# One-hot products of the mixture layers split into a rounded part and a rest, and three modulation parts of the third mixer summed on the vector engine

## The reference

```python
cond = jax.nn.silu(c)
for i in range(DEPTH):                     # layers 2 and 3 of the kernel
    sh1, sc1, g1, sh2, sc2, g2 = jnp.split(cond @ ada_w[i] + ada_b[i], 6, axis=-1)
    h = modulate(rmsnorm(x, norm_mix_g[i]), sh1, sc1)
    mix = gla_mixer(h, ...) if i % 2 == 0 else lru_mixer(h, ...)
    x = x + g1[:, None] * mix
    h = modulate(rmsnorm(x, norm_ffn_g[i]), sh2, sc2)
    x = x + g2[:, None] * grouped_moe(h, ...)

def grouped_moe(...):                      # combine: 2 of 16 experts per token
    for e in range(N_EXPERTS_2):
        he = jax.nn.silu(t @ w_gate[e]) * (t @ w_up[e])
        out = out + combine[:, e:e + 1] * (he @ w_down[e])
```

## Time and profile before

| | us |
|---|---|
| median of three runs | 2803.23 |
| lowest, highest | 2800.44, 2810.59 |
| the profiled execution: whole time | 2816.16 |
| its span, first to last instruction | 2814.4 |
| mean granted TensorE clock, of 2.4 GHz | 0.927 |
| third mixer, first slot to last modulation piece | 1744 to 1867 |
| mixture of layer 2, first gate product to last add | 1975 to 2291 |
| mixture of layer 3, the same | 2476 to 2801 |

### The profile page before, as it was taken

One profiled execution on the slowest core, in us unless ns is written; L12 is line 12 of the kernel. 1 busy time (PEld: TensorE's weight loads), 2 busy tenths in 40 slices (PEclk: granted clock), 3 DMA queues, 4 the chain that ended last, 5 costly groups with the idle time before them and its releaser, 6 DMA issues.

```text
span 2814.4 us, 26206 instructions
## 1 busy us (share of the span) xinstructions
PE 2422.6 (86%) x9674; PEld 1281.0 (46%) x9676; DVE 1169.7 (42%) x2825; ACT 625.0 (22%) x1780; POOL 644.9 (23%) x823
## 2 busy tenths in 40 slices
PE   6999888787778989977787788987999988799998
PEld 2577433333333567433333334346454456544544
DVE  0326666766664336667766763023100022320001
ACT  1112323322233122323332333111110022110101
POOL 1103433333332102433343331100222000012100
PEclk7989998899999999999899899987999999799999
DMA  8748999999997757999999997853899135579970
GB/s 328 301 171 332 416 421 422 421 422 421 421 422 314 286 207 312 417 422 421 422 421 422 421 421 328 312 204 135 359 421 421 70 135 201 247 307 421 421 299 16
DMA packets 130128, 934.40 MB, mean 332 GB/s; under 512 B 14288, under 2 KB 16336, under 8 KB 16592
## 3 DMA queue, kind: packets, MB, share of 16 engines
q0 software_dynamic: 114768, 835.96, 72.1%
q1 hardware_dynamic: 15232, 96.75, 8.8%
HBM read 1070.02 MB, written 1.05 MB: 381 GB/s over the span
## 4 chain that ended last, share of the span: by engine, by line
PE 54%; DMA 26%; DVE 15%; ACT 4%; issue 1%; SPq 0%; DVEq 0%; ACTq 0%
PE units L1101 15%; PE units L645 13%; DMA arena<-rows,idx 11%; PE accs L887 11%; DMA wide<-rows,idx 8%; DMA ring<-stream 5%; PE units L1079 3%; PE accs L1146 3%; DVE wide L1804 3%; DVE arena L1804 2%; PE units L660 2%; PE accs L725 2%; DMA wide<-experts 2%; ACT arena L1331 1%; DMA arena<-ada 1%
## 5 line engine op out<-in xcount | busy, mean ns | idle before, releaser
L887 PE MATMUL accs<-wide,arena 128*128 128x512 f32 x1040 | 518.7, 654 | 146.7 <-ACT arena L1331 144.9
L887 PE MATMUL accs<-arena 128*128 128x512 f32 x1008 | 482.7, 633 | 93.2 <-ACT arena L1331 93.2
L887 PEld LDWEIGHTS accs<-wide,arena 128*128 128x128 f32 x1040 | 211.3, 208 | 438.2 <-issue 254.3
L555 POOL DMA_INDIRECT wide<-rows,idx x260 | 245.0, 942 | 602.1 <-PE accs L887 422.0
L1101 PE MATMUL units<-wide,arena 128*64 128x512 f32 (+1 forms) x1728 | 368.1, 597 | 8.4 <-DMA wide<-experts 6.0
L887 PEld LDWEIGHTS accs<-arena 128*128 128x128 f32 x1008 | 203.1, 205 | 369.9 <-issue 248.8
L1199 ACT ACTIVATE arena<-units 128x512 f32<-128x512 f32 (+2 forms) x204 | 111.2, 559 | 1017.0 <-PE units L645 312.7
L645 PE MATMUL units<-arena,ring 128*128 128x256 f32 (+1 forms) x1344 | 300.2, 386 | 28.3 <-ACT arena L1226 14.0
L555 POOL DMA_INDIRECT arena<-rows,idx x252 | 237.3, 942 | 359.9 <-PE accs L887 322.1
L645 PEld LDWEIGHTS units<-arena,ring 128*128 128x128 f32 x1344 | 256.3, 200 | 74.2 <-issue 38.6
L1101 PE MATMUL units<-arena 128*64 128x512 f32 (+1 forms) x960 | 232.7, 593 | 0.5 <-ACT arena L1199 0.5
(11 more groups left out here) (301 smaller groups left out, 2102.1 us busy)
## 6 DMA issues: line engine op xcount, KB each, us to landing
wide<-experts POOLq DMA_DIRECT2D x123, 1024.0 KB, 13.4
wide<-experts SPq DMA_DIRECT2D x93, 1024.0 KB
wide<-ada POOLq DMA_DIRECT2D x88, 1024.0 KB, 9.2
arena<-experts POOLq DMA_DIRECT2D x69, 1024.0 KB, 16.2
ring<-stream SPq DMA_DIRECT2D x62, 1024.0 KB, 6.8
arena<-experts SPq DMA_DIRECT2D x51, 1024.0 KB
arena<-side SPq DMA_DIRECT2D x8, 1024.0 KB, 8.2
wide<-ada SPq DMA_DIRECT2D x7, 1024.0 KB, 16.9
```

What stands on the lines that cost most here:

```text
L555: pool.indirect_dma_start(row_slot(i), None, rows[l], bass.IndirectOffsetOnAxis(ap=idx[:, n, k:k + 1], axis=0)).then_inc(row_sem(i), 16)
L887: ins = mm(o[:, half * 512:(half + 1) * 512], diag[:, i % (2 * GROUP), :], row_slot(PICKS * l + i)[:, D + half * 512:D + (half + 1) * 512] ...
```

## The change

1. **Modulation parts of the third mixer.** `added(DEPTH)` names the three parts that PE took in `gla`. `add_piece` on DVE now multiplies each piece by its scalar of `cact` and adds it up in `ada_sums` (one tensor_scalar, then seven scalar_tensor_tensor of 2048 columns for each part), and a memset of one column releases the ring place. PE reads the sum with four matmuls against `one` (`sum_added`), after the first and second value pairs and after the gates. Parts 1 and 2 on DVE wait until PE has read the part before, since there is one `ada_sums`. That buffer is the seventh place: `ADA_RING` is 6 for every layer.
2. **One-hot products.** Tokens and the experts' results are stored as an f32r part (ACT writes it, rounded) and the rest, x minus that part (f32r too). The rest of the tokens is subtracted on POOL, between its 11th and 12th expert load; that of the results on DVE, in place of the copy. `place` and `add` run on both parts in f32r, so with twice as many matmuls, and `place` takes two tiles at a time: 32 matmuls of 256 columns at every second tile, into four units.
3. **The combine weight** goes into `h` (DVE's product becomes a scalar_tensor_tensor with a per-place scalar). The scalar comes from two one-column matmuls with `back` as weights; the scatter matrix is now `to` turned by two f32r matmuls against `ident_r`, not `back` by transposes. ACT takes both and does so one tile earlier than the tile that uses them (`turn_back(p + 1)`).

The diff, cut to its core:

```diff
-ADA_RING = 7
+ADA_RING = 6
+def added(l):
+    return ((l, 1), (l, 2), (l + 1, 0)) if l == DEPTH else ()
@@ POOL
             def expert_loads(l):
-                pool.wait_ge(ada_read, after_of(l))
+                for i in range(after_of(l) - ADA_RING, after_of(l)):
+                    pool.wait_ge(ada_free(i), ada_uses(i))
+                pool.wait_ge(ada_summed, sums_before(l + 1))
                 for i in range(OWN):
+                    if i == NE:
...
+                            pool.wait_ge(tok_hi_ready, 2 * TB * (l - DEPTH) + n + 1)
+                            wait_taken(pool, u)
+                            g.tensor_tensor(tok_lo[:, b, cut], tok[:, b, cut], tok_hi[:, b, cut].bitcast(F32),
+                                            ALU.subtract).then_inc(tok_lo_ready, 1)
@@ PE
+            def sum_added(l, j):
+                which, part = added(l)[j]
+                pe.wait_ge(ada_added, KT * (sums_before(l) + j + 1))
+                for g in range(4):
+                    ins = mm(ada_bank(which, part)[32 * g:32 * g + 32, :], one[:, 0:1].broadcast_to([P, 32]),
+                             ada_sums[:, g * 512:(g + 1) * 512], start=True, stop=True, skip_group_check=True)
+                ins.then_inc(ada_summed, 1)
-                token_slots(SLOT_OF["gk", l], UNIT_OF["gk", l], hT, adas=2)
+                token_slots(SLOT_OF["gk", l], UNIT_OF["gk", l], hT)
                 for c in range(2):
-                    token_slots(SLOT_OF["gv", l] + 2 * c, UNIT_OF["gv", l] + 2 * c, hT, adas=2)
+                    token_slots(SLOT_OF["gv", l] + 2 * c, UNIT_OF["gv", l] + 2 * c, hT)
+                    sum_added(l, c)
...
+                sum_added(l, 2)
+                def place(q):
+                    at = batch_tiles(q) * P
+                    for c, u in enumerate(batch_units(l, q)):
+                        open_bank(u)
+                        for j in range(2):
+                            k = 2 * c + j
                             for b in range(TB):
+                                for part, tok in enumerate(toks):
+                                    ins = mm(bank(u)[:, j * T:(j + 1) * T], tok[:, b, k * P:(k + 1) * P],
+                                             to[:, b, at:at + 2 * P], start=b + part == 0, stop=b + part == TB)
+                def turn_back(p):
+                    u = tile_units(l, p)["back"]
+                    open_bank(u)
+                    for b in range(TB):
+                        mm(bank(u)[:, b * P:(b + 1) * P], to[:, b, p * P:(p + 1) * P], ident_r[:, :], start=True, stop=True)
+                    for b in range(TB):
+                        ins = mm(bank(u)[:, T:T + 1], back[:, b, p * P:(p + 1) * P], one[:, :], start=b == 0, stop=b == TB - 1)
@@ add
                     for d in range(KT):
-                        ins = mm(acc[d // 2][:, (d % 2) * T:(d % 2 + 1) * T], o[:, d * P:(d + 1) * P], bT, ...)
+                        for part, o in enumerate(os):
+                            ins = mm(acc[d // 2][:, (d % 2) * T:(d % 2 + 1) * T], o[:, d * P:(d + 1) * P], bT, ...)
@@ the order on PE
-                for i in range(2 * TB):
-                    wait_taken(pe, UNIT_OF["tokens", l] + i)
+                pe.wait_ge(tok_lo_ready, 2 * TB * (l - DEPTH + 1))
                 pe.wait_ge(spread_ready, TB * (l - DEPTH + 1))
                 place(0)
+                pe.wait_ge(back_ready, l - DEPTH + 1)
+                turn_back(0)
...
+                    if p % 2 and p + 1 < TILES:
+                        place((p + 1) // 2)
                     if p + 1 < TILES:
-                        place(p + 1)
-                    transposes(q["back"], [back[:, b, p * P:(p + 1) * P] for b in range(TB)])
+                        turn_back(p + 1)
                     down(p)
@@ ACT
+                    for c, u in enumerate(q["down"]):
+                        wait_full(act, u)
+                        af(o_hi[:, c * 512:(c + 1) * 512], bank(u)[:, :], ACT.Copy).then_inc(o_hi_ready, 1)
@@ DVE
+            def add_piece(l, j, k):
+                if k == 0 and j:
+                    dve.wait_ge(ada_summed, sums_before(l) + j)
+                n = i - ADA_FIRST
+                dve.wait_ge(ada_landed[n % ADA_RING], 16 * (n // ADA_RING + 1))
+                if k == 0:
+                    ts(ada_sums, ada_piece(i), w, None, ALU.mult).then_inc(ada_added, 1)
+                else:
+                    stt(ada_sums, ada_piece(i), w, ada_sums, ALU.mult, ALU.add).then_inc(ada_added, 1)
+                v.memset(psr[:, k:k + 1], 0.0).then_inc(ada_free(i), 1)
-                    took(tt(h, si, bank(q["up"])[:, :], ALU.mult), q["up"])
+                    took(stt(h, si, wgt[:, p % 2, 0:1], bank(q["up"])[:, :], ALU.mult, ALU.mult), q["up"])
-                        took(v.tensor_copy(o[:, c * 512:(c + 1) * 512], bank(u)[:, :]), u)
+                        dve.wait_ge(o_hi_ready, 2 * (TILES * (l - DEPTH) + p) + c + 1)
+                        took(tt(o_lo[:, cut], bank(u)[:, :], o_hi[:, cut].bitcast(F32), ALU.subtract), u)
```

More of the change, by code:

```diff
@@ L66, with _tile_plan, take @@
 SIDE = (2, 3, 4, 5)
+BATCHES = (TILES + 1) // 2
+def _tile_plan():
+    n = 0
+    at = [{} for _ in range(TILES)]
+    batch = []
+    def take(k):
+        nonlocal n
+        n += k
+        return tuple(range(n - k, n))
+    batch.append(take(4))
+    at[0]["back"], = take(1)
+    for p in range(TILES):
+        (at[p]["gate"],), (at[p]["up"],), (at[p]["turn"],) = take(1), take(1), take(1)
+        if p % 2 and p + 1 < TILES:
+            batch.append(take(4))
+        if p + 1 < TILES:
+            at[p + 1]["back"], = take(1)
+        at[p]["down"] = take(2)
+    return at, batch, n
+TILE_AT, BATCH_AT, TILE_UNITS = _tile_plan()
 def plan():
@@ L138, in pieces, with sums_before, ada_uses @@
     return ((l, 1), (l, 2)) + (((l + 1, 0),) if l + 1 < LAYERS else ())
+def added(l):
+    return ((l, 1), (l, 2), (l + 1, 0)) if l == DEPTH else ()
+def sums_before(l):
+    return sum(len(added(n)) for n in range(l))
+def ada_uses(i):
+    return (i - ADA_FIRST) // ADA_RING + 2
 def before_of(l):
@@ L714, in ada_slots @@
             def ada_slots(n):
-                for i in range(ada_at[0], ada_at[0] + n):
+                todo = [i for i in range(ada_at[0], LAYERS * ADA_SLOTS) if not any(
+                    (i // ADA_SLOTS, i % ADA_SLOTS // KT) in added(l) for l in range(LAYERS))][:n]
+                ada_at[0] = todo[-1] + 1 if todo else ada_at[0]
+                for i in todo:
                     l, part, k = i // ADA_SLOTS, i % ADA_SLOTS // KT, i % KT
@@ L1116, in hidden @@
                     q, loads = tile_units(l, p), tile_loads(p)
-                    for c in range(2):
-                        wait_taken(pe, q["place"][c])
+                    half = p % 2 * P
+                    for u in batch_units(l, p // 2):
+                        wait_taken(pe, u)
                     for name, first in (("gate", 0), ("up", 2)):
```

157 lines of the change are left out of this document (107 added, 50 removed).

## The result

The changed kernel takes 2791.16 us (median of 9 runs, 2785.08 to 2800.45) and the kernel before 2809.06 (9 runs, 2800.44 to 2818.49): a ratio of 0.9939, 95% interval 0.9919 to 0.9959. It is faster by 0.6%, about 17 us. The forecast said 34, so its direction held and its size was twice what came.

A forecast was written before the change was run, and what follows sets the result against it. PE bounds the third mixer, with ring loads close behind; DMA paces the mixture's own tiles, and PE is alone behind the last load. -14.6 - 3.5 - 16.2 = -34 off the median 2803.2 gives 2769, by itself 2757 to 2783.

The forecast's parts named there:

- Part 3: Mixture of layers 2 and 3: one-hot products in f32r, 0.12 us per matmul of 256 columns; gain 16.2 in both.
- Costed at nothing: POOL's four subtractions: Head of the mixture: at most 5.2 us, ending at 1965, covered because PE waits for DVE until 1968.9.
- if PE waits at the head of the mixture for POOL's subtractions: Sign in the new profile, at the mixture's head, that the forecast is wrong altogether; no size given.
- Part 2: Modulation ring of six places: gain 3.5 us (0 to 4) in layer 1, together 0 in layer 3.
- one MB less is 2.5 us less: Start of layer 1: PE's wait of 2.67 nearly goes and the slot of 8.77 returns to 7.13; gain 3.5.
- Part 1: Third mixer: modulation parts moved from PE to DVE, stage from 122.6 to 108.0 us; gain 14.6.
- about 11 with a slower clock in one or two: Third mixer: five ring slots fall into the DMA backlog, 2 to 3 us each.
- The second reading: Third mixer: PE's wait before it 1 to 2 us; longer than 3 would mean DVE's chain was mis-sized.
- (a): Rival, one-hot products: f32r loads weights as slowly as f32, an add takes 3.8, total 2799; chance 0.12.
- (b): Rival, one-hot products: f32r runs at f32's speed, an add takes 6.9, total 2943; chance 0.07.
- (c): Rival, third mixer: every slot waits for its ring load while DVE adds, 9.5 to 10.2 each; 2783; chance 0.09.
- (d): Rival, own tiles: PE's clock stays down after waits, costing 5 to 7 us a layer; 2781; chance 0.06.

The follow-up runs named there:

- mix_only: The changed kernel with the mixture's one-hot products alone: modulation pieces all on PE again, ring of seven places; ratio to the kernel before 0.9963.
- keys_late: The changed kernel with layer 1's keys (1 MB) loaded behind all its modulation pieces instead of ahead of them; 2789.0 us, ratio 0.9932.
- sum_early: The changed kernel with PE's first reading of a sum two slots earlier and the second two slots later; 2789.4 us, ratio 0.9927.
- pace3: sum_early with at most three of the third mixer's 24 modulation pieces under way instead of six; 2790.07 us, ratio 0.9937.

## Why the forecast was right in direction and wrong in size

- **Part 3, the tiles: right.** The forecast's -9.0 behind the last load (its -8.1 without the +0.9 of the head) was -8.9 and -7.5 in the changed kernel's profile, -9.0 and -8.9 in mix_only's. Its prices hold: an add 2.10 (forecast 1.9), a gather 3.84 (3.8), the turning 0.57 (0.7).
- **Part 3, the head: the step that failed.** "Costed at nothing: POOL's four subtractions ... ends at 1965, and PE waits for DVE until 1968.9". The time was right (4.93 for at most 5.2) and the cover was wrong: it was DVE's routing that was to hide them, and DVE's routing is what they hold up. 3.35 per layer, 6.7 in all, shown by adding them alone and by taking them away. The text named the mark itself, "if PE waits at the head of the mixture for POOL's subtractions"; PE does, by way of DVE. The part's +0.9 for gather 0 and the turning was +1.9 and +0.9, with the low clock of gather 0 in it.
- **Part 2: the step "one MB less is 2.5 us less" failed.** 0.4 for 3.5. The first megabyte less shows in engines that have run empty by the time the load lands; a second one, in keys_late, gets 3.4. In layer 3 the forecast's 0 held: PE's wait of 1.65 is gone, the last piece comes later, and from the first slot to the first small matmul behind the last piece it is 103.0 for 103.7 (over all profiles 101.4 to 104.7 with six places and 103.7 to 104.6 with seven).
- **Part 1: the mechanism right, the size off.** 11.3 in the profiles for 14.6. The term that was mis-sized is "about 11 with a slower clock in one or two", which was to hold the waits and the slow slots behind them. It measured 15.3: waits of 11.0 (3.20, 4.75 and 3.07), 3.4 for two slow slots (1.6 at 1760.46, 1.7 at 1814.83) and 0.9 for the slow second reading. The 2.9 for the first pair was 2.8, and the other terms nearly cancel (twelve slots at full clock 84.2 for 85.6, the low-rank block 6.0 for 5.3). The term isn't large by bad luck: in keys_late the waits are 13.6 and a slow slot and reading 3.0. The second reading was named as the mark: over 3 us would mean DVE's chain was mis-sized, and it was 4.75. The text's own numbers gave 18.2 - 14.3 = 3.9, and took off 2 for loads that PE would wait for meanwhile; the two slots ran without a wait. A part took DVE 18.6 for 18.2, so it is the cover that was mis-sized and not DVE's chain. Averaged over the kernels the mixer takes 138.4 with PE's pieces (five kernels, 135.6 to 142.1) and 127.8 with DVE's sums (three), 10.6 less, and the medians leave 7. Between these the worth of the part stays open.
- **The rivals.** (a) and (b) are refuted by 2.10 for an add (they had 3.8 and 6.9). (c), the ring gives part 1 back, is right in kind: once PE no longer waits for DVE, the ring has the wait (sum_early), and four of its slots begin 10.2 to 11.2 after the one before them, but not every slot, and 20 us don't come back. (d) is refuted in its price: the granted clock is 1.00 in layer 2's own tiles, behind waits of 1.33, and the one slow expert product of layer 3 (6.31) was there in the kernel before (6.50). For (a) the text named the Trainium skill (TensorE: Matmul & The Clock Gate, on weight-path modes) and left open which side f32r stands on. Its weight loads are recorded with a median of 192 ns, about those of f32 in this trace (190 ns), and yet a product with weights of its own and 256 columns comes every 0.12 to 0.13. In the add at 2057.73 sixteen such loads keep PEld busy for 1.97 of the 2.10 us, so the records overlap each other, against the text's "but not each other", and their recorded length doesn't set the pace. No run tells which kind of weight load f32r gets.
- **The sum.** Forecast 34 = 14.6 + 3.5 + 16.2. Measured, by stages of the profiles from the norm of layer 2's mixer on: -11.2 to the recurrence, +1.3 behind it, -0.9 in layer 3's mixer, +6.7 norm to ranks, +2.8 ranks to first expert product, -16.3 in the tiles: -17.6. The largest single miss is the 6.7 of the heads, then 3.3 of part 1 and 3.1 of part 2. That the direction held is not luck: part 3, the larger one, gives 10 by itself. That 2791 lies in the range of 2752 to 2797 is: above the forecast's own 2783 the range was there for the better half of rival (a), which is refuted.

## What to carry to other kernels

Work is hidden by another engine's wait only if it doesn't hold up what that engine waits for: before costing an instruction of POOL at nothing, see whether DVE's small instructions with two SBUF inputs run beside it and whether somebody waits for them. Of a backlog in another queue only what is moved before the load lands seems to count: a first megabyte less brought 0.4 us here and the second 3.4. And where a stage is within some 20% of its bytes' time (some 90 of 111 us here, 36 MB at 421 GB/s), moving a wait from one engine to another returns little; the gain was in the two heads, where PE waited for a chain of instructions and nothing was being transferred for it.

## What was not expected of the hardware

- A DVE instruction of 0.17 us takes 0.92 to 1.00 when a POOL subtraction of 512 columns runs, and two of them 2.40 beside two; beside a memset it depends on the form: tensor_tensor 0.17, tensor_scalar 0.39 each, cast 0.42.
- A ring load of 1 MB beside a deep queue of POOL's takes 8.9 to 9.5, while the engines move some 3.8 MB at 420 GB/s (with seven places): it gets about a quarter of them, not half. The Trainium skill (DMA: Bandwidth & Descriptors, "Queues, rings and completion order") lets an engine take turns between its queues packet by packet; packets are about 7.3 KB in both queues here, so that, by an estimate from that rule, turns alone would give half. This trace doesn't agree. No run here shows where the rest goes. With three of POOL's pieces under way instead of six the middle landing in the third mixer is 6.7 (pace3), for 8.0 (sum_early).
- f32r products of 256 columns come every 0.12 to 0.13 us with weights of their own, one record each, where an f32 product took 0.46 in two records.
- The same small matmuls of layers 0 and 1 took 5.47 or 10.34 in kernels whose code there is nearly the same, so that 5 us between two single profiles can come from this group alone.
